# Bias and selection mask of a sparse attention added on TensorE by a product with the identity

## The chip, the cores and the metric

The kernel runs on one core of one Trainium2 chip. The metric is the device time of one execution in microseconds (us); the number given for a kernel is the median of several runs. The engines are called PE (TensorE, with PEld for its weight loads), DVE (VectorE), ACT (ScalarE), POOL (GpSimd) and SP (SyncE).

## The reference, cut to what matters

Two transformer blocks follow one another on 512 tokens of width 1024. The second has a sparse attention of 8 heads over a shared latent of 128 values. For each query the 128 keys with the best index score are selected, a bias by distance is added to the logits, and keys not selected or not causal are masked:

```python
logits = (einsum('bqhc,bqkc->bqhk', ql, c_sel) * ATT_SCALE + bias)
logits = where(valid[:, :, None, :], logits, -inf)
probs = softmax(logits, axis=-1)
return einsum('bqhk,bqkc->bqhc', probs, c_sel)
```

The kernel computes this densely: all causal keys of a block of 128 queries take part, and a mask of 0 (selected) or a huge negative number (not selected) is added.

## The kernel before, in words

All matrices are kept transposed, with features in the 128 partitions and the 512 tokens (T) along the free axis. The large projections are products in three parts: each weight chunk is split by ACT into a rounded half w_hi (line 1197) and by DVE or POOL into the rest w_lo (POOL: line 655), and PE runs w_hi·a_hi, w_hi·a_lo and w_lo·a_hi (lines 765 to 767 for chunks that fill gaps in other work, 743 to 745 elsewhere). The work of every engine is in program order, with semaphores between engines.

The change lies in the loop over the steps of the sparse attention, from 1187 to 1282 us of the span. There are 32 steps a = 0 to 31: 8 heads h = a // 4 times 4 query blocks i = a % 4. Block i has (i+1)·128 keys, so that the width of a step goes 128, 256, 384, 512. Each engine walks the same loop with a lag of its own:

- POOL (lines 696 to 714): one add per step makes bias_mask = t_bias + score for step a (line 708). There are two buffers, held in the tiles sum_sq and diagonal, so step a waits until step a-2 has been used. t_bias is loaded by a DMA that ACT issues, once per head (line 1455). Behind the add stands, in some steps, the split of a weight unit (w_lo, line 655).
- PE (lines 1052 to 1092): the logits of step a (line 1059, into one of three rotating "aux" banks), then the transposes of the probabilities of step a-2 (line 1066, i+1 blocks, which wait for DVE's attn2), then one or two chunks of a gate projection that fill the time (765 to 767; a third product closes a tile and releases one unit of weights), then the products with the values of step a-3 (line 1080), and in four steps (11, 19, 27, 35) the products of line 1090.
- DVE (lines 2278 to 2318): the add of step a, logit = bank + bias_mask (line 2286), which also sets the bank free; the reciprocal of the sum of step a-1 (2291); the maximum of logit of step a (2294) and its negation (2295), for which ACT waits; the scaling attn2 = prob · 1/sum of step a-1 (2303), for which PE's transposes of the next step wait.
- ACT (lines 1525 to 1560): the copy of the transposed probabilities of step a-2 (1530), the exponential of step a with its sum (1538, it is followed by a short row that reads the accumulator), then w_hi of a unit whose tile has closed, the copy of that tile (1470), and once per head the copy of the head's output (1552).

The aux banks are handed out in the order in which PE uses them: logit a, turn2 a-2 (the transposes), logit a+1, turn2 a-1, and so on, with an entry "ya" at the four steps of line 1090. An entry may be written when the entry three places before has been read. So turn2 a-1 takes the bank of logit a, and after a "ya" entry logit a+1 takes the bank of logit a.

Before the loop DVE selects the keys of block 1 (16 rounds of line 2205 and 2206, up to 1187 us), and POOL ends the splits of the units before (the last one runs from 1184.67 us). After the loop comes a recurrence in which DVE, ACT, POOL and PE take turns, filled with further chunks of the gate projection.

Of the kernel before, what the change touches and what calls it, by code (L numbers as in the profile page):

```python
# [34 lines left out]
ALU = mybir.AluOpType  # L35
# [3 lines left out]
P = 128  # L39
T = 512  # L40
# [277 lines left out]
def two_blocks(nc, ins, spill, bias_rows, out):  # L318

    with ExitStack() as ctx:  # L320
# [109 lines left out]
        qa = r2_under("qa", [P, 2, T])  # L430
        relu = r2_under("relu", [P, 2, T])
        i_t = r2_under("i_t", [P, 2, T])
        logit = r2("logit", [P, 2, T])
        prob2 = r2("prob2", [P, 2, T])
        attn2 = r2("attn2", [P, 2, T])
        after_steps = r2.at[0]
# [80 lines left out]
        def sem(name):  # L517
            return ctx.enter_context(nc.semaphore(name))
# [48 lines left out]
        spill_out = [sem(f"spill_out{i}") for i in range(2)]  # L567
        bias_in = [sem(f"bias_in{i}") for i in range(2)]
        logit_max = sem("logit_max")
        exp2_done = sem("exp2_done")  # L570
        attn2_ready = sem("attn2_ready")
        hq_loaded = [sem(f"hq_loaded{i}") for i in range(2)]
        hf_loaded = [sem(f"hf_loaded{i}") for i in range(2)]
# [74 lines left out]
        @block.gpsimd  # L648
        def _(pool):
            def split_unit(u, size, it=0, per_loop=0):  # L650
                slot, half = u % SLOTS, u % SLOTS
                hi, lo, src = w_hi[:, half, 0:size], w_lo[:, half, 0:size], raw[:, slot, 0:size]

                pool.wait_ge(unit_high, u + 1 + it * per_loop)
                pool.tensor_tensor(lo, src, hi.bitcast(F32), ALU.subtract).then_inc(unit_split, 1)  # L655

            def split_units(name, start, end):

                first, size = UNIT[name][0], UNIT[name][2] * P
                loops = max(0, end - start) // SLOTS  # L660
                if loops > 1:
                    with pool.Fori(0, loops) as it:
                        for j in range(SLOTS):
                            split_unit(first + start + j, size, it, SLOTS)
                    start += SLOTS * loops
                for i in range(start, end):
                    split_unit(first + i, size)

            def split_for(t):

                u = UNIT["proj2"][0] + t + 3
                split_unit(u, BLOCKS_OF[u] * P)

            def make_diff(e):

                h, l = e // len(LEVELS), e % len(LEVELS)
                b = LEVELS[l]
                if l == 0:
                    pool.wait_ge(sums_ready, h + 1)
                if e >= 2:  # L680
                    pool.wait_ge(decay_ready, decays((e - 2) // len(LEVELS), (e - 2) % len(LEVELS)))
                src = run[h % 2][:, max(0, l - 6), :].rearrange("p (n c) -> p n c", c=2 * b)
                to = diff[:, e % 2, :].rearrange("p (n c) -> p n c", c=2 * b)
                mid = src[:, :, b - 1:b].broadcast_to([P, T // (2 * b), b])
                ins_ = pool.tensor_tensor(to[:, :, 0:b], mid, src[:, :, 0:b], ALU.subtract)
                if b <= 32:
                    ins_ = pool.tensor_tensor(to[:, :, b:2 * b], src[:, :, b:2 * b], mid, ALU.subtract)
                ins_.then_inc(diff_ready, 1)

            split_units("proj1", 0, UNIT["proj1"][1])  # L690
            split_units("wo", 0, SLOTS)
            pool.wait_ge(unit_split, UNIT["proj2"][0] + SLOTS)
            split_units("proj2", SLOTS, LEAD2 + 3)

            pool.wait_ge(const2_loaded, 16 * 3)
            pool.wait_ge(rstd_ready, STAT["kidx"] + 1)
            for a in range(DSA_STEPS + 4):
                if a < DSA_STEPS:
                    h, i = a // QB, a % QB
                    end, first_col = (i + 1) * P, (QB - 1 - i) * P  # L700
                    if i == 0:
                        pool.wait_ge(bias_in[h % 2], 16 * (h // 2 + 1))
                    if a == 1:
                        pool.wait_ge(selected_ready, 3)
                    if a >= 2:
                        former = aux_read("logit", a - 2)
                        pool.wait_ge(former[0], former[1])
                    pool.tensor_tensor(bias_mask[a % 2][:, 0:end], t_bias[:, h % 2, first_col:first_col + end],
                                       score[i][:, :], ALU.add).then_inc(bias_mask_ready, 1)
                if a >= 3:  # L710
                    for t in closed(FILL2[a - 3]):
                        split_for(t)

            make_diff(0)
            for e in range(HGRN_STEPS):
                if e + 1 < HGRN_STEPS:
                    make_diff(e + 1)
# [3 lines left out]
        def _(pe):  # L721
# [331 lines left out]
            for a in range(DSA_STEPS + 4):  # L1053
                if a < DSA_STEPS:
                    h, i = a // QB, a % QB
                    end = (i + 1) * P
                    dst = aux_wait("logit", a)
                    wait(aux_read("qlat", h))
                    mm(dst[:, 0:end], qlat[:, h, i * P:end], ckv[:, 0:end], start=True,
                       stop=True).then_inc(aux_ready, 1)  # L1060
                if 2 <= a < DSA_STEPS + 2:
                    b = a - 2
                    dst = aux_wait("turn2", b)
                    pe.wait_ge(attn2_ready, b + 1)
                    for j in range(b % QB + 1):
                        step = pe.transpose(dst[:, j * P:(j + 1) * P], attn2[:, b % 2, j * P:(j + 1) * P],
                                            ident[:, :])
                    step.then_inc(aux_ready, 1)
                if a < DSA_STEPS + 3:
                    fill("proj2", FILL2[a])  # L1070
                if 3 <= a < DSA_STEPS + 3:
                    b = a - 3
                    h, i = b // QB, b % QB
                    if i == 0:
                        wait_bank("olat", h)
                        wait(aux_read("ckvtok", 0))
                    wait(aux_read("turn2", b))
                    dst = tile_bank("olat", h)
                    for j in range(i + 1):
                        step = mm(dst[:, i * P:(i + 1) * P], ckv_tok[:, j, :],  # L1080
                                  attn2_t[:, b % 2, j * P:(j + 1) * P], start=(j == 0), stop=(j == i))
                    if i == QB - 1:
                        step.then_inc(head_ready, 1)
                if a >= 11 and a % 8 == 3:
                    t = (a - 11) // 8
                    dst = aux_wait("ya", t)
                    wait(tile_read("olat", 2 * t))
                    wait(tile_read("olat", 2 * t + 1))
                    for n in range(2):
                        step = mm(dst[64 * n:64 * n + 64, :], wuv[:, 2 * t + n, :], olat[:, n, :], start=True,  # L1090
                                  stop=True)
                    step.then_inc(aux_ready, 1)
# [92 lines left out]
        def _(act):  # L1185
# [339 lines left out]
            for a in range(DSA_STEPS + 4):  # L1525
# [6 lines left out]
                if a < DSA_STEPS:  # L1532
# [2 lines left out]
                    act.wait_ge(logit_max, a + 1)  # L1535
                    if a >= 2:
                        act.wait_ge(attn2_ready, a - 1)
                    fn(prob2[:, a % 2, 0:end], logit[:, a % 2, 0:end], ACT.Exp,
                       bias=small[:, 24 + a % 2:25 + a % 2],
                       accum_out=small[:, 26 + a % 2:27 + a % 2]).then_inc(exp2_done, 1)  # L1540
                    if i == 1 and 1 <= h < DSA_HEADS - 1:
                        act.wait_ge(bias_mask_ready, QB * h)
                        load_bias(h + 1)
# [168 lines left out]
        def _(dve):  # L1712
# [565 lines left out]
            for a in range(DSA_STEPS + 4):  # L2278
                if a < DSA_STEPS:
                    h, i = a // QB, a % QB  # L2280
                    end, s = (i + 1) * P, a % 2
                    dve.wait_ge(bias_mask_ready, a + 1)
                    dve.wait_ge(aux_ready, AUX["logit", a] + 1)
                    if a >= 2:
                        dve.wait_ge(exp2_done, a - 1)
                    v.tensor_tensor(logit[:, s, 0:end], aux_bank("logit", a)[:, 0:end], bias_mask[s][:, 0:end],
                                    ALU.add).then_inc(aux_sem("logit", a), 1)
                if 1 <= a <= DSA_STEPS:
                    r = (a - 1) % 2
                    dve.wait_ge(exp2_done, a)  # L2290
                    step(v.reciprocal(small[:, 28 + r:29 + r], small[:, 26 + r:27 + r]))
                if a < DSA_STEPS:
                    wait(aux_read("logit", a))
                    step(v.tensor_reduce(small[:, 6:7], logit[:, s, 0:end], AX_X, ALU.max))
                    v.tensor_scalar(small[:, 24 + s:25 + s], small[:, 6:7], -1.0, None, ALU.mult).then_inc(
                        logit_max, 1)
                if 1 <= a <= DSA_STEPS:
                    b = a - 1
                    end, s = (b % QB + 1) * P, b % 2
# [250 lines left out]
```

## Time and profile before

| | before |
|---|---|
| median of 3 runs | 1962.74 us (1958.37 to 1964.58) |
| time of the profiled execution | 1960.72 us |
| its span | 1958.6 us |
| PE busy | 1836.3 us (94% of the span) |
| PEld busy | 1486.7 us (76%) |
| DVE busy | 1140.8 us (58%) |
| ACT busy | 657.1 us (34%) |
| POOL busy | 204.5 us (10%) |
| mean granted clock of TensorE | 0.972 |

A busy share is time in which at least one instruction of the engine is recorded as running. Matmuls are pipelined: a row of PE begins when the operands begin to stream in, and its recorded end overlaps with the next row, so the time that a matmul takes from the engine is read from the distance between two starts. The stage of the change takes 95 us of the 1958.6.

### The profile page before, as it was taken

The page shows a single profiled execution, that of the slowest core. Times are in us where ns is not written, and L with a number is a line of the kernel's source. Part 1 is how long each engine was busy: PE and PEld are TensorE (multiplying, and loading weights), DVE is VectorE, ACT ScalarE, POOL GpSimd, SP SyncE. Part 2 cuts the span into 40 slices and gives each one's busy share as a digit, 9 for nine tenths or more (in the row PEclk, how much of TensorE's full clock was granted, in tenths as well). Part 3 has the DMA queues.
Part 4 walks back from the last instruction along what each step waited for, and adds up shares of the span by engine and source line. Part 5 has one row for each costly group of instructions (what it writes and reads, how often), then busy time and mean ns, then how long its engine had stood idle before and what let it go on. Part 6 is the DMA issues. An engine that isn't in the chain of part 4 may idle for free.

```text
span 1958.6 us, 23662 instructions
## 1 busy us (share of the span) xinstructions
PE 1836.3 (94%) x8380; PEld 1486.7 (76%) x8380; DVE 1140.8 (58%) x1721; ACT 657.1 (34%) x978; POOL 204.5 (10%) x150
## 2 busy tenths in 40 slices
PE   6996999999999999999999998888898999999986
PEld 4675888888888888888776776667776888888864
DVE  6466668888334655532343777788666655552256
ACT  4333422333223222222333334444444322232242
POOL 3221000000000000000023334444000000000000
PEclk9997999999999999999899999999999999999998
DMA  4676222223322232333222333221241323332221
GB/s 141 71 75 49 86 97 96 96 96 104 102 91 79 97 96 96 100 103 104 80 76 76 105 123 118 69 88 43 93 153 56 108 96 96 96 119 101 90 67 54
DMA packets 55460, 180.62 MB, mean 92 GB/s; under 512 B 6336, under 2 KB 7104, under 8 KB 55392
## 3 DMA queue, kind: packets, MB, share of 16 engines
q1 hardware_dynamic: 43200, 157.07, 24.3%
q10 hardware_dynamic: 12192, 22.67, 7.2%
q8 instruction: 40, 0.66, 0.1%
q14 instruction: 28, 0.23, 0.0%
HBM read 167.65 MB, written 12.06 MB: 92 GB/s over the span
## 4 chain that ended last, share of the span: by engine, by line
PE 77%; DVE 14%; ACT 3%; issue 3%; DMA 2%; ACTq 0%; DVEq 0%; SPq 0%; POOL 0%
PE bank L743 20%; PE bank L744 20%; PE bank L745 20%; PE bank L765 2%; PE bank L767 2%; PE bank L766 2%; PE bank L839 2%; PE bank L840 1%; PE bank L841 1%; DVE score L2206 1%; DMA raw<-in_w_proj 1%; DVE best L2205 1%; PE bank L814 1%; PE bank L1132 1%; DVE chunk L1872 1%
## 5 line engine op out<-in xcount | busy, mean ns | idle before, releaser
L1197 ACT ACTIVATE w_hi<-raw 128x1024 fp32r<-128x1024 f32 (+2 forms) x281 | 304.6, 1087 | 743.7 <-PE bank L745 640.8
L743 PE MATMUL bank<-a_hi,w_hi 128*128 128x512 f32 x1272 | 500.6, 394 | 14.6 <-DVE w_lo L1775 4.9
L745 PE MATMUL bank<-a_hi,w_lo 128*128 128x512 f32 x1272 | 496.6, 390 | 0.0
L744 PE MATMUL bank<-a_lo,w_hi 128*128 128x512 f32 x1272 | 496.6, 390 | 0.0
L1775 DVE TENSOR_TENSOR w_lo<-raw,w_hi 128x1024 fp32r<-128x1024 f32 (+2 forms) x219 | 280.4, 1281 | 253.8 <-ACT w_hi L1197 241.2
L743 PEld LDWEIGHTS bank<-a_hi,w_hi 128*128 128x128 f32 x1272 | 239.7, 188 | 76.8 <-issue 18.9
L745 PEld LDWEIGHTS bank<-a_hi,w_lo 128*128 128x128 f32 x1272 | 239.6, 188 | 50.7
L744 PEld LDWEIGHTS bank<-a_lo,w_hi 128*128 128x128 f32 x1272 | 240.0, 189 | 48.8
L655 POOL TENSOR_TENSOR w_lo<-raw,w_hi 128x1024 fp32r<-128x1024 f32 x54 | 130.0, 2408 | 1071.3 <-ACT w_hi L1197 1071.3
L743 PE MATMUL bank<-h_hi,w_hi 128*128 128x512 f32 x568 | 221.0, 389 | 0.0
L744 PE MATMUL bank<-h_lo,w_hi 128*128 128x512 f32 x568 | 221.0, 389 | 0.0
L745 PE MATMUL bank<-h_hi,w_lo 128*128 128x512 f32 x568 | 220.9, 389 | 0.0
L745 PEld LDWEIGHTS bank<-h_hi,w_lo 128*128 128x128 f32 x568 | 106.6, 188 | 22.2
L743 PEld LDWEIGHTS bank<-h_hi,w_hi 128*128 128x128 f32 x568 | 106.6, 188 | 22.2
L744 PEld LDWEIGHTS bank<-h_lo,w_hi 128*128 128x128 f32 x568 | 106.6, 188 | 22.1
L765 PE MATMUL bank<-a_hi,w_hi 128*128 128x512 f32 x234 | 104.9, 448 | 3.4 <-ACT unrot L1311 3.4
L2123 DVE TENSOR_TENSOR val<-bank,rstd 128x512 f32<-128x512 f32 x44 | 30.4, 691 | 114.3 <-PE bank L745 114.3
L767 PE MATMUL bank<-a_hi,w_lo 128*128 128x512 f32 x234 | 95.1, 406 | 0.0
L766 PE MATMUL bank<-a_lo,w_hi 128*128 128x512 f32 x234 | 95.0, 406 | 0.0
L839 PE MATMUL bank<-a_hi,w_hi 128*128 128x512 f32 x150 | 64.9, 433 | 30.2 <-DVE a_lo L1781 28.6
L839 PEld LDWEIGHTS bank<-a_hi,w_hi 128*128 128x128 f32 x150 | 30.3, 202 | 43.6 <-DVE a_lo L1781 27.8
L840 PE MATMUL bank<-a_lo,w_hi 128*128 128x512 f32 x150 | 61.9, 413 | 0.0
(297 smaller groups left out, 2210.6 us busy)
## 6 DMA issues: line engine op xcount, KB each, us to landing
raw<-in_w_up SPq DMA_DIRECT2D x132, 512.0 KB, 3.4
raw<-in_w_down SPq DMA_DIRECT2D x48, 704.0 KB, 4.1
raw<-in_w_proj SPq DMA_DIRECT2D x59, 512.0 KB, 3.5
raw<-in_w_wo SPq DMA_DIRECT2D x8, 512.0 KB, 4.8
raw<-in_w_branch SPq DMA_DIRECT2D x16, 256.0 KB, 2.8
gates_in<-spill ACTq DMA_DIRECT2D x16, 256.0 KB, 3.2
raw<-in_w_out SPq DMA_DIRECT2D x8, 512.0 KB, 3.9
raw<-in_w_ple SPq DMA_DIRECT2D x8, 512.0 KB, 3.4
```

The lines of the kernel that those rows point to most:

```text
L655: pool.tensor_tensor(lo, src, hi.bitcast(F32), ALU.subtract).then_inc(unit_split, 1)
L743: mm(dst[:, :], wh, hi[:, k, :], start=(first and c == 0), stop=False)
L744: mm(dst[:, :], wh, lo[:, k, :], start=False, stop=False)
L745: step = mm(dst[:, :], wl, hi[:, k, :], start=False, stop=(last and c == n - 1))
L765: mm(dst[:, :], wh, a_hi[:, c, :], start=(c == 0), stop=False)
L766: mm(dst[:, :], wh, a_lo[:, c, :], start=False, stop=False)
L767: step = mm(dst[:, :], wl, a_hi[:, c, :], start=False, stop=(c == DC - 1))
L839: mm(dst[:, :], wh, hi[:, k, :], start=(k == 0), stop=False)
L840: mm(dst[:, :], wh, lo[:, k, :], start=False, stop=False)
L1197: fn(w_hi[:, slot, 0:size], raw[:, slot, 0:size], ACT.Copy).then_inc(unit_high, 1)
L1775: v.tensor_tensor(w_lo[:, slot, 0:size], raw[:, slot, 0:size], w_hi[:, slot, 0:size].bitcast(F32), ALU.subtract).then_inc(unit_split, 1)
L2123: v.tensor_tensor(val[:, :], bank[u][:, :], rstd[:, :], ALU.mult).then_inc(bank_free[u], 1)
```

## The change

POOL, PE, DVE and ACT are touched. On PE the logits of line 1059 are left open in the bank, and a second product, with the identity as the stationary and bias_mask as the moving operand, is added to the same bank. DVE has no add any more and takes the maximum straight from the bank; ACT's exponential reads the bank too and now sets it free. The tile logit is gone (its room stays reserved). POOL's wait for the buffer of step a-2 is now for PE's product instead of DVE's add. On DVE the maximum and its negation now stand ahead of the reciprocal.

```diff
@@ POOL
                     if a >= 2:
-                        former = aux_read("logit", a - 2)
-                        pool.wait_ge(former[0], former[1])
+                        pool.wait_ge(aux_ready, AUX["logit", a - 2] + 1)
@@ PE
                     wait(aux_read("qlat", h))
-                    mm(dst[:, 0:end], qlat[:, h, i * P:end], ckv[:, 0:end], start=True,
+                    mm(dst[:, 0:end], qlat[:, h, i * P:end], ckv[:, 0:end], start=True, stop=False)
+                    pe.wait_ge(bias_mask_ready, a + 1)
+                    mm(dst[:, 0:end], ident[:, :], bias_mask[a % 2][:, 0:end], start=False,
                        stop=True).then_inc(aux_ready, 1)
@@ ACT
-                    fn(prob2[:, a % 2, 0:end], logit[:, a % 2, 0:end], ACT.Exp,
+                    fn(prob2[:, a % 2, 0:end], aux_bank("logit", a)[:, 0:end], ACT.Exp,
                        bias=small[:, 24 + a % 2:25 + a % 2],
-                       accum_out=small[:, 26 + a % 2:27 + a % 2]).then_inc(exp2_done, 1)
+                       accum_out=small[:, 26 + a % 2:27 + a % 2]).then_inc(aux_sem("logit", a), 1)
@@ DVE
-                    dve.wait_ge(bias_mask_ready, a + 1)
                     dve.wait_ge(aux_ready, AUX["logit", a] + 1)
+                    step(v.tensor_reduce(small[:, 6:7], aux_bank("logit", a)[:, 0:end], AX_X, ALU.max))
                     if a >= 2:
-                        dve.wait_ge(exp2_done, a - 1)
-                    v.tensor_tensor(logit[:, s, 0:end], aux_bank("logit", a)[:, 0:end], bias_mask[s][:, 0:end],
-                                    ALU.add).then_inc(aux_sem("logit", a), 1)
+                        wait(aux_read("logit", a - 2))
+                    v.tensor_scalar(small[:, 24 + s:25 + s], small[:, 6:7], -1.0, None, ALU.mult).then_inc(
+                        logit_max, 1)
                 if 1 <= a <= DSA_STEPS:
                     r = (a - 1) % 2
-                    dve.wait_ge(exp2_done, a)
+                    wait(aux_read("logit", a - 1))
                     step(v.reciprocal(small[:, 28 + r:29 + r], small[:, 26 + r:27 + r]))
-                if a < DSA_STEPS:
-                    wait(aux_read("logit", a))
-                    step(v.tensor_reduce(small[:, 6:7], logit[:, s, 0:end], AX_X, ALU.max))
-                    v.tensor_scalar(small[:, 24 + s:25 + s], small[:, 6:7], -1.0, None, ALU.mult).then_inc(
-                        logit_max, 1)
```

## Rows read from the trace of the kernel before

**Rows 1.** Windows: us, busy (rows) of each engine, granted clock, DMA share, GB/s

```profile
1187.00:1282.00 95.00, 79.88 (x430) 61.06 (x430) 66.89 (x171) 46.52 (x116) 37.61 (x37) 0.95 0.24 82
...
1187.00:1196.40 9.40, 5.39 (x15) 3.59 (x16) 6.68 (x21) 2.93 (x9) 4.54 (x7) 0.64 0.04 14
...
1230.47:1240.66 10.19, 10.19 (x57) 7.55 (x58) 7.42 (x21) 4.72 (x13) 3.90 (x5) 1.00 0.12 34
...
1261.90:1275.87 13.97, 10.67 (x54) 8.39 (x52) 9.26 (x21) 6.00 (x16) 4.74 (x3) 0.88 0.05 20
```

**Rows 2.** Waits, 1187 to 1282 us: us in total, times, longest us

```profile
PE bank L1066 <- DVE attn L2303: 15.6, 11, 4.4
```

**Rows 3.** Timeline of PE, steps 7 and 8: start us, us, line, operation, [idle before]

```profile
1203.17 1.02 PE L1059 MATMUL bank<-ckv,qlat 128*128 128x512 f32 x2
1204.03 0.38 PE L1066 MATMUL bank<-ident,attn 128*128 128x128 f32 x2
1204.17 0.48 PE L765 MATMUL bank<-a_hi,w_hi 128*128 128x512 f32 x1
...
1204.95 0.38 PE L1080 MATMUL bank<-attn_t,ckv_tok 128*128 128x128 f32 x2
1205.17 0.39 PE L1059 MATMUL bank<-ckv,qlat 128*128 128x128 f32 x2
1206.57 0.52 PE L1066 MATMUL bank<-ident,attn 128*128 128x128 f32 x3 [1.01 <-DVE attn L2303]
```

**Rows 4.** Timeline of DVE, ACT and POOL in the same steps

```profile
1204.40 0.69 DVE L2286 TENSOR_TENSOR logit<-bank,diagonal 128x512 f32<-128x512 f32 x1 [0.87 <-PE bank L1059]
...
1205.19 0.69 DVE L2294 TENSOR_REDUCE small<-logit 128x1 f32<-128x512 f32 x1
...
1206.00 0.42 DVE L2303 TENSOR_SCALAR attn<-prob,small 128x384 f32<-128x384 f32 x1
...
1207.91 2.67 DVE L2303 TENSOR_SCALAR attn<-prob,small 128x512 f32<-128x512 f32 x1
...
1206.10 0.73 ACT L1538 ACTIVATE prob<-logit,small 128x512 f32<-128x512 f32 x1 [1.27 <-DVE small L2295]
...
1206.83 1.04 ACT L1197 ACTIVATE w_hi<-raw 128x1024 fp32r<-128x1024 f32 x1
...
1206.56 0.46 POOL L708 TENSOR_TENSOR sum_sq<-t_bias,tri 128x128 f32<-128x128 f32 x1 [5.39 <-DMA t_bias<-bias_rows]
...
1207.95 2.34 POOL L655 TENSOR_TENSOR w_lo<-raw,w_hi 128x1024 fp32r<-128x1024 f32 x1 [0.22 <-ACT w_hi L1197]
```

**Rows 5.** Groups by shape: busy us, mean ns

```profile
L2286 DVE TENSOR_TENSOR logit<-bank,diagonal 128x512 f32<-128x512 f32 x8 | 5.5, 692 | 9.3 <-PE bank L1059 9.3
L2294 DVE TENSOR_REDUCE small<-logit 128x1 f32<-128x512 f32 x8 | 5.5, 686 | 0.3
...
L1538 ACT ACTIVATE prob<-logit,small 128x512 f32<-128x512 f32 x8 | 5.8, 724 | 8.7 <-DVE small L2295 8.7
```

**Rows 6.** The same, in the first attention, which reads its banks directly

```profile
L1988 DVE TENSOR_REDUCE small<-bank 128x1 f32<-128x512 f32 x8 | 5.5, 692 | 1.9 <-PE bank L956 1.7
...
L1334 ACT ACTIVATE prob<-bank,small 128x512 f32<-128x512 f32 x8 | 5.5, 688 | 14.6 <-DVE small L1989 14.3
```

**Rows 7.** Timeline at the start of the loop: PE, then POOL

```profile
1185.38 0.81 PE L1059 MATMUL bank<-ckv,qlat 128*128 128x384 f32 x2
1190.59 0.45 PE L1066 MATMUL bank<-ident,attn 128*128 128x128 f32 x1 [4.41 <-DVE attn L2303]
...
1195.60 0.39 PE L1059 MATMUL bank<-ckv,qlat 128*128 128x128 f32 x2
...
1186.99 0.51 POOL L708 TENSOR_TENSOR sum_sq<-t_bias,tri 128x128 f32<-128x128 f32 x1
```

**Rows 8.** Timeline of steps 28 and 29: PE's wait, DVE's scaling before it

```profile
1266.03 0.63 PE L1066 MATMUL bank<-ident,attn 128*128 128x128 f32 x4 [2.06 <-DVE attn L2303]
...
1263.60 2.28 DVE L2303 TENSOR_SCALAR attn<-prob,small 128x512 f32<-128x512 f32 x1
```

More of the change, by code:

```diff
@@ L432, in two_blocks @@
         i_t = r2_under("i_t", [P, 2, T])
-        logit = r2("logit", [P, 2, T])
+        r2.at[0] += 2 * T * 4
         prob2 = r2("prob2", [P, 2, T])
@@ L569, in two_blocks @@
         logit_max = sem("logit_max")
-        exp2_done = sem("exp2_done")
         attn2_ready = sem("attn2_ready")
```

## The prediction

> **What bounds the kernel now.** I read the page first (PE is busy in all but 6% of the span), then the windows of the stage that is changed, its waits, and the timeline of each engine in it. The windows show two things [rows 1]. Over the stage's 95 us the recorded PE time is 79.9 us, more than DVE's 66.9, ACT's 46.5 or POOL's 37.6. And there is a head, 1230.47 to 1240.66 us, in which PE's rows touch one another for all 10.19 us. The waits name one thing that PE waits for: DVE's attn2 ahead of the transposes, 15.6 us in 11 waits, the longest (4.4 us) at the start of the loop [rows 2]. So the stage is PE's own work, with ten waits of 11.2 us together behind a chain on DVE and one longer wait at the start. PE's clock fell in two places: 0.64 granted in the first 9.4 us, and 0.88 in the last 13.97 us [rows 1], which is 13.97 · 0.12 = 1.7 us lost.
>
> The chain behind a wait, in steps 7 and 8 [rows 4]: logits of step 7 end, add 0.69, reciprocal, maximum 0.69, negation, attn2 of step 6 0.42, and only then PE's transposes at 1206.57 [rows 3]. The gap shown is 1.01, but by starts it is 1206.57 - 1205.17 less the 0.22 that a product of 128 columns takes, so 1.2. Corrected so (some 0.17 for each of ten), the ten waits are worth 12.9 us.
>
> **The change, part by part.**
>
> *The product with the identity (PE, on the path).* It has the shape of the product of line 1059. That one takes 1204.03 - 1203.17 = 0.86 us for 512 columns, two rows [rows 3], so 0.215 for each 128. A head adds 1 + 2 + 3 + 4 = 10 such pieces, 2.15 us; steps 4 to 31 add 7 · 2.15 = **+15.05 us**. A head without waits goes from 10.19 to 12.3. Bounds: if it ran in one row for each block, as the transposes with the identity do (1204.17 - 1204.03 = 0.14 for two blocks [rows 3], or 0.07; other transposes of the trace take up to 0.11), it would be half, +7.5; above, half clock as in the first stretch would double what falls into it. I take 0.215, since the moving operand is not transposed and the instruction is that of line 1059 but for its operands.
>
> *The add that goes (DVE).* 0.69 us at 512 columns [rows 5], less at fewer (0.29 at 128). It is off the path where PE doesn't wait; where it does, the chain is shorter by the add of the step before. *Maximum and exponential from the bank:* the first attention does just that. The maximum takes 692 ns there against 686, the exponential 688 against 724 [rows 5, 6]. Both count as nothing (between -0.04 and +0.01 each).
>
> *Which of the waits are left.* PE comes later to its transposes by the new products, DVE is ready earlier. From the end of the products of a step with 512 columns, attn2 of the step before was ready after 1206.57 - 1204.03 = 2.5 us [rows 3]. Without the add it would be 1.8. But the transposes also need the bank of that step's logits, and it now comes free after the exponential: latency 0.35, maximum 0.7, negation and hand-over 0.3, exponential with its accumulator 0.85, so 2.2 to 2.3 us. PE meanwhile has two transposes, a chunk, and values, logits and mask of a 128 step: 1205.17 - 1204.03 = 1.14, and 2 · 0.22, so 1.57. A wait of **0.7** stays, in steps 4, 8, 16, 24 and 32, 3.5 us. In steps 12, 20 and 28 the products of line 1090 stand before it and cover it. The waits in steps 9, 21, 13 and 22 go: PE arrives later by 0.66 to 1.1 us and DVE is ready 0.3 to 0.7 sooner.
>
> *POOL's splits.* attn2 of step 7 took 2.67 us for 512 columns beside a POOL split of 2.34 [rows 4], and in step 28 2.28 [rows 8]; it seems to wait the split out. The split follows ACT's exponential and w_hi (exponential at 1206.10, w_hi 1206.83, split 1207.95 [rows 4]). With the change exponential and split are both 0.7 earlier against the logits. For step 7 I get attn2 from 2.6 to 3.1 us behind the products and the split from 3.35, so no collision (by 0.25 us); for step 28, where DVE copies ya first, attn2 still falls into the split, and a wait of about **1.2** is left of 2.06 [rows 8]. Left in all: 3.5 + 1.2 = 4.7 of 12.9, so **-8.2 us**.
>
> *Clock.* With the wait of step 29 down to 1.2, what PE did before the fall in the last stretch is gone; I count the **-1.7**, and 0 as the other end.
>
> *The start.* This is the new wait. Before, PE ran logits 0 to 2 with their chunks up to 1186 us, while DVE was still selecting, and then stood until 1190.59. Now it stands in front of the first mask product until POOL's first add at 1186.99 + 0.51 = 1187.5 [rows 7]; behind it in PE's queue stand all chunks, logits 1 and 2 and the first transposes. They were done for nothing before. PE has stood 4 us, so I take it to run at half clock for some 4.5 us behind it again: the 0.64 over the first 9.4 us [rows 1] is 6.8 us at half clock, part of it standing. Then: mask 0 0.44, chunk 1.28, logits and mask 1 1.76, chunk 1.28, logits and mask 2 1.3 at full clock, transposes of step 0 at 1193.6, chunk, logits and mask 3 to 1196.1, transposes, chunk, values, logits and mask 4 to 1197.65. Logits 4 ended at 1195.8 before [rows 7]. Less the 0.22 of mask 4, already counted, that is **+1.6 us** (bounds: 0 if the clock stays up, +3).
>
> *POOL's new wait.* It starts its add 0.3 us sooner behind the logits than behind DVE's add, and PE needs the result two steps later, 5 us. Hidden. The one tight place is mask 8: its bias arrived after 5.39 us of waiting, at 1206.56 [rows 4], after PE's logits 8 but before its next transposes. The loads stand behind four others that ACT issues in step 4, which comes 1.5 us later now, and PE reaches mask 8 at some 1209.0, POOL has it at 1208.5. Hidden by half a microsecond; if not, PE stands here with everything behind it.
>
> *Sum:* 15.05 - 8.2 - 1.7 + 1.6 = +6.75, about **+7 us**. On the profiled execution's 1960.72 us that is 1967.7. It lies 2 us below the median of 1962.74, so that the forecast for a median is **1969.7 us**.
>
> **Rivals.**
>
> *PE has room (not slower).* All ten waits vanish and the start costs nothing: the new products fall into time in which PE stood. Then 15.05 - 12.9 - 1.7 = +0.5, 1963 us. It decides where the bank comes free before PE arrives, that is if the exponential of a 512 step ends within 1.6 us of its products instead of 2.3. For it speaks that weight loads fill only 61.06 of 95 us [rows 1]. The Trainium skill (Perfetto Trace Analysis, Identifying the Most-Contended Engine) would have PE's headroom judged by the share of weight loads and by arithmetic, not by matmul busy time; by that PE would have a third to spare and the change would fit in. Against it speaks the head of 10.19 us: weight loads are 7.55 us of it, 74%, and yet no row of PE starts late [rows 1]. Chance 0.27.
>
> *Half-price product (not slower).* One row instead of two, -7.5 from the sum: 1962. Chance 0.05.
>
> *PE stands for POOL or ACT (much slower).* The mask comes late in PE's queue: mask 8 behind its DMA, or a mask behind a split of 2.3 us; or ACT, with w_hi, the tile copy and the head's copy in one step (1.0 + 0.6 + 0.6), starts the next exponential late and holds the bank. Each such place costs 1 to 2 us where it hits, and four or five steps have a split: +6 more, and the fallen clock is not won back (+1.7). 1975 to 1978 us. For it: the long wait of POOL for its DMA [rows 4]; against it: two steps of lead. Chance 0.14.
>
> *DVE's chain rules the stage (faster).* Only if waits were due in most steps; then the 15.6 us of adds would come off and the products would be in the shade: -7 us. The gap-free head speaks against it. Chance 0.04.
>
> **How the numbers follow.** The forecast, +4 to +10 us, has 0.5 of the chance. 0.3% of this kernel, 5.9 us, is about what its runs can tell from no change, and lies just below the sum. Of the forecast some two thirds lie above it; the first two rivals lie within it, the third above. That gives slower 0.56, same 0.39, faster 0.05. The range goes from 1963 (PE has room) to 1976 (forecast plus a few places where PE stands); the forecast's own range is 1966.5 to 1973.
>
> **What the profile would show.** The product of the new line as two rows of 0.43 each for 512 columns, some 17 us of starts in all. PE's stretch from the first transposes of head 1 to those of head 7 longer by about its share. The wait of line 1066 down from 15.6 us in 11 to some 5 in 6, in steps with i = 0, and put down to ACT's exponential as much as to attn2. A new wait of PE of about 4 us for POOL at 1183.6. The last logits products of the loop ending near 1281 instead of 1273. I would be wrong if DVE's waits on the path outlast the removed add (collisions with POOL at new places), if the clock falls anew, or if the mask product shows waits for POOL after step 3.

## The result, and the profile after

The changed kernel takes 1965.74 us as the median of 16 runs (1962.59 to 1968.82), the kernel before 1962.44 us in 16 runs beside it (1956.13 to 1964.58). The ratio is 1.0025, with a 95% interval of 1.0014 to 1.0036: slower by 5 us, 3 to 7 (the two medians alone are 3.3 us apart). The prediction was +7, a median of 1969.7 and a range of 1963 to 1976.

The windows of the changed kernel, for the 95 us of the stage and for the 103 that it takes now (columns as in rows 1):

```profile
1187.00:1282.00 95.00, 90.49 (x463) 67.19 (x464) 44.10 (x134) 41.47 (x108) 39.28 (x37) 0.98 0.24 83
1187.00:1290.00 103.00, 97.14 (x504) 72.83 (x504) 50.07 (x145) 47.53 (x118) 39.28 (x37) 0.98 0.24 82
```

Against [rows 1], over the whole stage (95 us before, 103 now), DVE fell from 66.9 to 50.1 us and PE rose from 79.9 to 97.1. The engine with room lost work and the one without got it. The granted clock of the stage rose from 0.95 to 0.98: the fall in the last stretch is gone, the one at the start has stayed (below).

The waits of the changed kernel from 1175 to 1290 us, those that bear on PE and on the new hand-overs:

```profile
POOL sum_sq L706 <- DMA t_bias<-bias_rows: 11.4, 5, 4.9
...
PE bank L1059 <- POOL sum_sq L706: 3.8, 1, 3.8
...
PE bank L1066 <- DVE attn L2298: 1.2, 2, 0.7
PE bank L1066 <- ACT prob L1538: 1.1, 4, 0.3
```

PE's waits at the transposes, 15.6 us in 11 before [rows 2], are 2.3 in 6 (1.2 and 1.1 in the last two lines). In their place stands one wait of 3.8 us for POOL. Here it is in PE's timeline, with the first transposes and what runs at half clock between them:

```profile
1185.31 0.38 PE L1057 MATMUL bank<-ckv,qlat 128*128 128x128 f32 x2
1189.50 0.49 PE L1059 MATMUL bank<-sum_sq,ident 128*128 128x128 f32 x2 [3.81 <-POOL sum_sq L706]
...
1190.96 1.05 PE L1057 MATMUL bank<-ckv,qlat 128*128 128x256 f32 x2
1191.81 1.06 PE L1059 MATMUL bank<-diagonal,ident 128*128 128x256 f32 x2
...
1195.00 0.27 PE L1066 MATMUL bank<-ident,attn 128*128 128x128 f32 x1
...
1198.66 0.39 PE L1057 MATMUL bank<-ckv,qlat 128*128 128x128 f32 x2
```

A product of 256 columns takes 1191.81 - 1190.96 = 0.85 us here, 0.43 later. The windows say why (columns as in rows 1, first a stretch of the changed kernel, then its loop behind the start, then the last stretch of the kernel before):

```profile
1190.00:1193.00 3.00, 3.00 (x8) 2.36 (x8) 0.47 (x3) 0.46 (x2) 1.16 (x3) 0.50 0.00 0
1198.90:1291.00 92.10, 87.74 (x473) 66.11 (x471) 44.88 (x125) 44.19 (x109) 32.69 (x30) 1.00 0.25 84
...
1266.03:1270.00 3.97, 3.97 (x16) 3.44 (x17) 1.98 (x5) 1.09 (x3) 1.96 (x2) 0.60 0.02 4
```

The granted clock is 0.50 there, the lower level of 1.2 GHz, shortly after PE stood for 3.8 us. Behind the start it is 1.00 up to 1291 us. Before, it was 0.60 once more in the 4 us behind the wait of step 29 [rows 8]. Steps 7 and 8 in the changed kernel, PE:

```profile
1207.39 1.02 PE L1057 MATMUL bank<-ckv,qlat 128*128 128x512 f32 x2
1208.26 1.02 PE L1059 MATMUL bank<-diagonal,ident 128*128 128x512 f32 x2
1209.11 0.38 PE L1066 MATMUL bank<-ident,attn 128*128 128x128 f32 x2
...
1210.25 0.39 PE L1057 MATMUL bank<-ckv,qlat 128*128 128x128 f32 x2
1210.47 0.39 PE L1059 MATMUL bank<-sum_sq,ident 128*128 128x128 f32 x2
1211.13 0.55 PE L1066 MATMUL bank<-ident,attn 128*128 128x128 f32 x3 [0.27 <-ACT prob L1538]
```

And DVE, ACT and POOL beside them:

```profile
1209.38 0.69 DVE L2283 TENSOR_REDUCE small<-bank 128x1 f32<-128x512 f32 x1 [2.21 <-PE bank L1059]
...
1211.55 0.49 DVE L2298 TENSOR_SCALAR attn<-prob,small 128x512 f32<-128x512 f32 x1
...
1210.30 0.69 ACT L1538 ACTIVATE prob<-bank,small 128x512 f32<-128x512 f32 x1 [0.38 <-DVE small L2286]
1210.88 0.19 ACT L1538 ACTIVATION_READ_ACCUMULATOR prob<-bank,small 128x1 f32 x1
...
1209.09 0.46 POOL L706 TENSOR_TENSOR sum_sq<-t_bias,tri 128x128 f32<-128x128 f32 x1 [4.95 <-DMA t_bias<-bias_rows]
...
1212.10 2.36 POOL L654 TENSOR_TENSOR w_lo<-raw,w_hi 128x1024 fp32r<-128x1024 f32 x1 [1.86 <-ACT w_hi L1197]
```

The new product takes 1209.11 - 1208.26 = 0.85 us for 512 columns, and 0.22 for 128 (from 1223.63 to the next start at 1223.85). The transposes after it wait 0.27 by the row (0.44 by starts), and what they wait for is ACT's exponential, which sets the bank free at 1211.07. attn2 of step 7 runs at 1211.55 in 0.49 us, against 2.67 before [rows 4]; it is done before POOL's split starts at 1212.10.

To leave out what happens ahead of the stage I take times from the first logits (1183.33 us before, 1185.31 after) to the last products of line 1090 (1283.70 and 1291.25): 100.4 us before, 105.9 after, **+5.6 us**. The 2 us between the two starting points are no part of the change. Over the twelve profiles of the versions below, whose code up to there is the same on PE, the first logits start anywhere from 1181.4 to 1186.8. The time from those last products to the end of the span scatters too, from 673 to 678 us.

### The profile page after: what moved, and what is told of

Its sections match the earlier page's. It is cut to its first block, busy times and chain, and to the rows that moved or that the text cites. A ratio compares the mean times of both kernels' runs of the same rounds, so it can differ in the third digit from the quotient of the medians.

```text
span 1965.1 us, 23727 instructions
## 1 busy us (share of the span) xinstructions
PE 1852.9 (94%) x8444; PEld 1498.4 (76%) x8444; DVE 1121.5 (57%) x1689; ACT 656.4 (33%) x978; POOL 204.1 (10%) x150
## 4 chain that ended last, share of the span: by engine, by line
PE 79%; DVE 12%; ACT 3%; issue 3%; DMA 2%; POOL 0%; ACTq 0%; DVEq 0%; SPq 0%; POOLq 0%
PE bank L741 20%; PE bank L742 20%; PE bank L743 20%; PE bank L763 2%; PE bank L764 2%; PE bank L765 2%; PE bank L837 2%; PE bank L838 1%; PE bank L839 1%; DMA raw<-in_w_proj 1%; PE bank L812 1%; PE bank L779 1%; DVE chunk L1872 1%; DVE x L1874 1%; PE bank L1132 1%
```

## The experiments

All stand on one of the two kernels. "Stretch" is the time just defined, from the run's own profile. Each ratio is to runs of the kernel before on the same chip. The runs were made on several chips (the kernel before had medians from 1960.8 to 1963.1 on them), so medians of different rows are compared more safely by their ratios.

| run | median us | ratio to before, 95% interval | stretch us |
|---|---|---|---|
| before | 1962.44 | | 100.4 |
| changed | 1965.74 | 1.0025 (1.0014 to 1.0036) | 105.9 |
| e1 changed, no product | 1951.35 | 0.9942 (0.9925 to 0.9960) | 91.8 |
| e2 changed, logits twice | 1980.26 | 1.0092 (1.0061 to 1.0123) | 121.1 |
| e3 before, logits twice | 1969.34 | 1.0040 (1.0021 to 1.0059) | 108.6 |
| e4 changed, mask 0 early | 1963.85 | 1.0008 (0.9990 to 1.0027) | 106.1 |
| e5 before, scaling first | 1955.36 | 0.9965 (0.9951 to 0.9979) | 95.6 |
| e5b the same again | 1955.70 | 0.9968 (0.9953 to 0.9983) | 96.3 |
| e6 changed, scaling first | 1965.03 | 1.0020 (1.0005 to 1.0035) | 105.8 |
| e7 changed, mask in fp32r | 1956.95 | 0.9975 (0.9963 to 0.9986) | 96.4 |
| e8 e7, mask 0 early | 1956.78 | 0.9970 (0.9954 to 0.9986) | 97.8 |
| e9 e7, scaling first | 1957.24 | 0.9970 (0.9959 to 0.9982) | 96.6 |
| e10 e8, loads later | 1956.84 | 0.9980 (0.9967 to 0.9993) | 98.0 |
| e11 e4, loads later | 1965.85 | 1.0022 (1.0009 to 1.0035) | 106.0 |

Ratio and stretch do not always give the same difference to the kernel before. For e3 they agree (+7.8 us and +8.2). For e1 they are -11.4 and -8.6, for e8 -5.9 and -2.6, for e4 +1.6 and +5.7. The stretch is one profile of each version, and e5 and e5b, the same code, differ by 0.7 us in it. So what is said below of single microseconds rests on single waits in single profiles.

### e1: the product taken out

The logits get neither bias nor mask here, so the kernel leaves out a part of the work; PE's wait for the mask goes with the product.

```diff
-                    mm(dst[:, 0:end], qlat[:, h, i * P:end], ckv[:, 0:end], start=True, stop=False)
-                    pe.wait_ge(bias_mask_ready, a + 1)
-                    mm(dst[:, 0:end], ident[:, :], bias_mask[a % 2][:, 0:end], start=False,
-                       stop=True).then_inc(aux_ready, 1)
+                    mm(dst[:, 0:end], qlat[:, h, i * P:end], ckv[:, 0:end], start=True,
+                       stop=True).then_inc(aux_ready, 1)
```

> The changed kernel without the product with the identity and without its wait for the mask; the logits get neither bias nor mask, POOL's adds still run. Theory A (PE's own time rules the stage, the product costs 0.215 us for each 128 columns): some 12 us under the changed kernel, and 8 us under the kernel before, since the add's share of the waits is gained and nothing is paid: PE's waits in the loop fall from 12.9 us to 6 or 7, the fallen clock of the last stretch is not there, so about 1954 us. Rival B (PE has room, the product falls into its waits): within 2 us of the changed kernel, 1963 to 1966. Rival D (DVE's chain rules): also about the changed kernel.

Measured: 1951.35 us, 14.4 under the changed kernel and 11 under the one before by the medians. PE's waits in it, 1175 to 1300 us:

```profile
PE bank L1065 <- DVE attn L2297: 6.5, 5, 3.2
...
PE bank L1065 <- ACT prob L1537: 1.5, 3, 0.6
```

The product and its wait for the mask cost 105.9 - 91.8 = 14.1 us of the stretch, where the product takes 17.2 from PE; so it is not hidden. The other half of the change, the add off DVE and both reads from the bank, is worth 8.6 us by itself (100.4 to 91.8). About 1.6 of them are the clock, which is 1.00 in the last 28 us of e1's stretch and was 0.60 for 4 us before. I had expected 12 and 8.

### e2 and e3: PE's share doubled on both kernels

```diff
+                    mm(dst[:, 0:end], qlat[:, h, i * P:end], ckv[:, 0:end], start=True, stop=True)
...
```

> The changed kernel with the product of the logits issued twice (the second overwrites the first): PE gets 8 times 2.15 = 17.2 us more, nothing else changes. Theory A: hardly a wait is left to take it up (some 3 us), so +13 to +16 us on the changed kernel, 1979 to 1982. Rival B: under +5.

> The kernel before with the product of the logits issued twice: the change's price on PE without what it takes from DVE, from POOL's order and from the start. Theory A: 17.2 us more, of which 2 fall into the standing time at the start, about 5 into the ten waits, and 1.7 come back from the clock: +8 to +10, 1971 us, so 4 to 5 us above the changed kernel, which is what the add on DVE is worth less the new wait at the start. Rival B: the waits of 12.9 us take it all up, +2. Rival D: +2 as well, since the chain on DVE is as long as before.

e2 took 14.5 us more than the changed kernel. From the first logits to the last transposes its profile has 114.8 us against 99.6, so 15.2 of the 17.2 us are paid. e3 took 6.2 us more than the kernel before by the medians, 7.8 by the ratio and 8.2 by the stretch. The waits there take up the other half: the same work added on PE costs 8 us where PE has 11 us of waits in the loop, and 15 where it has 2. e3 has PE's part of the change without DVE's, and lies 2.6 us of stretch above the changed kernel: that is what the add on DVE is worth once PE is full, net of the new wait at the start. I had expected 4 to 5.

### e4: the mask of step 0 ahead of POOL's last split

```diff
-            split_units("proj2", SLOTS, LEAD2 + 3)
+            split_units("proj2", SLOTS, LEAD2 + 2)
...
+            pool.wait_ge(bias_in[0], 16)
+            pool.tensor_tensor(bias_mask[0][:, 0:P], t_bias[:, 0, (QB - 1) * P:QB * P], score[0][:, :],
+                               ALU.add).then_inc(bias_mask_ready, 1)
+            split_units("proj2", LEAD2 + 2, LEAD2 + 3)
             for a in range(DSA_STEPS + 4):
-                if a < DSA_STEPS:
+                if 0 < a < DSA_STEPS:
```

> The changed kernel with POOL's add of step 0 ahead of its last split before the loop, so that PE's first mask product finds its mask. Theory A: PE's wait of 3.8 us shrinks, it goes on to logits 1 and then waits for mask 1, which can only follow the selection that DVE ends at about 1187: 1 to 2 us less than the changed kernel, 1964 to 1965. If the start cost nothing (rival B): no difference.

The median is 1963.85, but the stretch is no shorter. PE's waits in it, 1175 to 1300 us:

```profile
PE bank L1063 <- POOL diagonal L710: 2.9, 1, 2.9
...
PE bank L1070 <- DVE attn L2302: 2.1, 3, 0.8
PE bank L1070 <- ACT prob L1542: 0.9, 3, 0.3
PE bank L1063 <- POOL sum_sq L710: 0.6, 1, 0.6
```

The first transposes come 8.7 us after the first logits instead of 9.7. The gain of 1 us is given back in step 8, where PE now stands 0.6 us for mask 8 (the last row), whose bias comes by DMA, and another 0.8 for attn2 in the step after. So the early mask shortens the wait at the start by 0.9 us, from 3.8 to 2.9, and later steps lose that again. A start without any wait was not tried. The interval of e4's ratio overlaps that of the changed kernel: within the measurement the two are the same.

### e5 and e6: DVE's scaling ahead of its add or maximum

```diff
+                if 1 <= a <= DSA_STEPS:
+                    r = (a - 1) % 2
...
+                    step(v.reciprocal(small[:, 28 + r:29 + r], small[:, 26 + r:27 + r]))
...
+                    v.tensor_scalar(attn2[:, s, 0:end], prob2[:, s, 0:end], small[:, 28 + s:29 + s], None,
+                                    ALU.mult).then_inc(attn2_ready, 1)
                 if a < DSA_STEPS:
                     h, i = a // QB, a % QB
...
-                    step(v.reciprocal(small[:, 28 + r:29 + r], small[:, 26 + r:27 + r]))
...
-                    v.tensor_scalar(attn2[:, s, 0:end], prob2[:, s, 0:end], small[:, 28 + s:29 + s], None,
-                                    ALU.mult).then_inc(attn2_ready, 1)
```

> The kernel before with DVE's reciprocal and scaling of step a-1 ahead of its add of step a, so that the transposes never wait for the add and the maximum. If the add and the maximum ahead of attn2 are the whole of the ten waits, they go: -10 us, 1952. But the loop then has DVE and ACT in one ring (exponential, reciprocal, scaling, add, maximum, negation, exponential): by the rows some 3.0 + 0.8 + 3.0 + 1.95 + 1.95 + 0.6 us for a head and 1.2 of hand-overs, 12.5 us, against 10.2 of PE's own work and 11.3 measured. By that it is slower, up to +9, 1971. I hold the second for likelier.

> The changed kernel with the same order on DVE. The ring without the add is 10.5 us for a head, under PE's 12.3, so it doesn't rule. Theory A says that the waits that are left in steps 4, 8, 16, 24 are for the bank, which ACT's exponential frees, not for attn2: then nothing changes, within 1.5 us of the changed kernel. If they were for attn2 they would go: -2 us.

e5 is 6.5 us faster than the kernel before, and I had held it for slower. The groups of the scaling by shape in e5, 1183 to 1280 us:

```profile
L2289 DVE TENSOR_SCALAR attn<-prob,small 128x512 f32<-128x512 f32 x8 | 4.6, 571 | 0.6 <-PE bank L1059 0.3
...
L2289 DVE TENSOR_SCALAR attn<-prob,small 128x128 f32<-128x128 f32 x8 | 3.0, 374 | 0.3
```

and in the kernel before, 1183 to 1282 us:

```profile
L2303 DVE TENSOR_SCALAR attn<-prob,small 128x512 f32<-128x512 f32 x8 | 9.3, 1160 | 0.0
L2303 DVE TENSOR_SCALAR attn<-prob,small 128x128 f32<-128x128 f32 x8 | 8.5, 1067 | 0.0
```

Wherever in the fourteen profiles no row of POOL is beside it, a scaling takes 0.29, 0.35, 0.42 or 0.49 us, by its width. Longer rows stand only where a row of POOL overlaps. Before, 19 of the 32 scalings overlap one, all eight of 128 columns among them; in e5 it is 8 of 32, and all scalings together fall from 24.7 to 14.0 us.

My sum for the ring of DVE and ACT, 12.5 us for a head, was too long. The scalings of 512 and 128 columns take (1160 - 571) + (1067 - 374) ns = 1.3 us of it away, which leaves 11.2, but two heads, from 1236.05 to 1256.36, take 10.2 us each, PE's own time [rows 1]. Summing recorded lengths counted too much: the scaling at 1238.37 is recorded with 0.49 us, and the next row of DVE starts 0.40 after it.

Not all of the gain comes from POOL. Of the ten waits of the loop before, six (7.5 us) stand behind a scaling that overlaps POOL, and four (3.7 us) behind one of 0.42 us that overlaps nothing; there the add and the maximum stand ahead of the scaling, as in steps 7 and 8 [rows 4]. The clock is 1.00 in e5's last 27 us, which is worth another 1.6. How the gain divides among the three was not measured. By the stretch it is 4.8 us, and 4.1 in e5b, not 6.5; where the rest lies is open. e5b, with the kernel before run beside it again, confirms the time:

> The kernel before with the scaling ahead of the add once more, on the same chip as the run beside it, to tell which of the two is faster. From its first run 1955.4; the same within 2 us as the run beside it.

In e6 the same order brings nothing (105.8 against 105.9 us of stretch), as expected. Of PE's waits that are left in the changed kernel those of 0.3 us in steps 4, 8, 16 and 24 are for the bank. In e6 they are 0.2, and in step 8 it is the mask that comes last. The two for attn2, 1.2 us in steps 29 and 32, do go, but PE then stands 1.2 us for the bank in step 29.

### e7 to e9: a cheaper product

The mask buffers and a copy of the identity are typed fp32r (the mask and the bias are rounded so), and the product has one row instead of two:

```diff
-                    mm(dst[:, 0:end], ident[:, :], bias_mask[a % 2][:, 0:end], start=False,
+                    mm(dst[:, 0:end], ident_r[:, :], bias_mask[a % 2][:, 0:end], start=False,
```

> The changed kernel with mask and identity held as fp32r, so that the product takes one pass of 0.23 us for 512 columns as those of lines 763 to 765 do, and not 0.86 (the mask and the bias are rounded so far). Theory A: PE gets 8 times 0.57 us and some 0.1 us for each change of kind, 7.8 us in place of 17.2; some waits come back. 1956 to 1959 us, 7 to 9 under the changed kernel and under the one before too. Rival C (PE stands for POOL or ACT in these steps): no gain, since the waits would stay.

> The same, and POOL's add of step 0 ahead of its last split as well. Theory A: 1 to 2 us under the run before it, 1955 to 1957.

> The changed kernel with the mask product in fp32r and with DVE's reciprocal and scaling ahead of the maximum. In the fp32r kernel PE still waits for attn2 3.3 us in 4 waits and for the bank 1.3 us in 3 inside the loop. Theory A: the scaling, moved ahead, no longer falls into POOL's splits, the waits for attn2 go and those for the bank stay or grow a little: 1 to 3 us under it, 1954 to 1956. If the waits for attn2 turn into waits for the bank: no difference.

PE's timeline of steps 7 and 8 in e7:

```profile
1201.38 1.02 PE L1062 MATMUL bank<-ckv,qlat 128*128 128x512 f32 x2
1201.84 0.80 PE L1066 MATMUL bank<-bias_mask,ident_r 128*128 128x512 f32 x1
1202.47 0.38 PE L1073 MATMUL bank<-ident,attn 128*128 128x128 f32 x2
```

Logits and mask take 1.09 us together where they took 1.72: the mask's part is 1.09 - 0.86 = 0.23. The kernel is 8.8 us faster than the changed one and 5 faster than the one before. That is the prediction's sum with one term exchanged, and the best evidence that this term was the price. By starts the mask's part is 0.23, 0.17, 0.12 and 0.06 us for the four widths, so 4.6 us in eight heads in place of 17.2. PE's waits by the rows grow from 6.1 to 9.0, and 12.6 - 2.9 = 9.7 is what the stretch shows: 105.9 - 96.4 = 9.5. e8 and e9 bring nothing more in the median, and e8's stretch is 1.5 us longer: in e8 the microsecond won at the start is lost to a wait of 1.8 us for mask 8, in e9 the waits for attn2 (3.3 us in 4) become waits for the bank (3.5 us in 6).

### e10 and e11: the loads out of the way of mask 8

```diff
-                if a == 4:
+                if a == 6:
```

> The fp32r kernel with mask 0 early, and ACT's six loads of step 4 (resets, masks, two forget and two query tiles) issued in step 6, behind the load of the bias of head 2 instead of ahead of it. Theory A: in the run without this PE stood 1.8 us for mask 8, whose bias comes behind these loads; that wait goes, 1 to 2 us less, about 1955. Rival: the 1.1 us won at the start are lost to the waits for the bank and for attn2, whatever mask 8 does: then no difference and no wait for POOL in step 8.

> The changed kernel (product in full precision) with mask 0 early and the same loads in step 6. PE's waits of 0.62 for mask 8 and of 0.82 for attn2 in step 9 (0.28 of bank time in the changed kernel) go back: PE's stretch from the first logits to the last products of line 1090 is 105.0 us instead of 106.1, about 1964 us.

Both missed. The wait for mask 8 went, and PE's waits in e11, 1175 to 1300 us, have it in another place:

```profile
PE bank L1063 <- POOL diagonal L710: 3.0, 1, 3.0
...
PE bank L1070 <- ACT prob L1542: 2.0, 4, 1.1
PE bank L1070 <- DVE attn L2302: 1.2, 2, 0.7
```

What holds the bank is ACT. Here are its rows in e10 (ACTq is its queue as it issues a DMA) and PE's wait:

```profile
1205.80 0.34 ACTq L1565 DMA_DIRECT2D resets<-in_c_resets  x1
...
1209.22 0.63 ACTq L1525 DMA_DIRECT2D hq<-spill  x1
1209.90 0.38 ACT L1541 ACTIVATE attn_t<-bank 128x256 f32<-128x256 f32 x1 [3.52 <-issue]
1210.18 0.68 ACT L1549 ACTIVATE prob<-bank,small 128x512 f32<-128x512 f32 x1
...
1211.01 0.55 PE L1077 MATMUL bank<-ident,attn 128*128 128x128 f32 x3 [2.75 <-ACT prob L1549]
```

The six loads are issued from 1205.80 to 1209.85. DVE's negation for step 7 had run at 1207.68, but the exponential starts only at 1210.18. So now the exponential of step 7 comes late and holds the bank: 1.1 us in e11, 2.75 in e10. The issues take ACT's queue 4.0 us in e10, 3.2 in e11 and 3.1 in the kernel before (1197.50 to 1200.57). The cost of the bundle is ACT's time in this loop. A place for it outside the loop was not tried.

## Why the prediction was right

The direction, the cause and most terms held. The total of +7 was 1 to 2 us too high, by the stretch (+5.6) and by the ratio (+5). The median of 1965.74 lies 4 us under the 1969.7 forecast and just under the forecast's own range, 1966.5 to 1973; it is inside the wide range that the rivals had made.

- *The product on PE.* 0.215 us for each 128 columns, forecast from line 1059, measured 0.85 for 512. Right, and e1, e2 and e7 show that it is the price: 14.1 to 15.2 us of the 17.2 are paid. The half-price rival is out: the product is two rows.
- *The waits that are left.* Forecast 0.7 in each of steps 4, 8, 16 and 24, covered in 12, 20 and 28, by the bank and not by attn2. Measured 0.44 by starts in exactly those four, put down to ACT's exponential. I had put the bank's release at 2.2 to 2.3 us behind the products; it is 1211.07 - 1209.11 = 1.96. The last one (step 32) is 0.7 as forecast, that of step 29 0.9 instead of 1.2, and 0.3 came up in step 9. In all 3.6 instead of 4.7 of 12.9. This was the mis-sized term.
- *The collisions with POOL's split.* attn2 of step 7 was to be done at 3.1 us behind the products and the split to start at 3.35; it is 2.93 and 2.99. Right in sign by 0.06 us, which is luck: it could have gone the other way. In step 28 attn2 fell into the split as forecast (2.06 us from 1272.18, beside the split at 1271.58).
- *The clock.* The fall in the last stretch is gone: the granted clock is 1.00 from 1198.90 to 1291.00. Whether the shorter wait in step 29 alone did it is not shown.
- *The start.* Forecast a wait of 4 us and a loss of 1.6; measured 3.8 and, at the end of mask 4 against logits 4, 13.8 - 12.5 us from the first logits less the 0.22 of mask 4, so 1.1. The clock was back after 3.6 us, not 4.5.
- *Sum by measured terms.* 15.05 - 9.3 - 1.7 + 1.1 = 5.2, against 5.6 in the stretch.
- *The chances.* They do not follow from their parts. Two thirds of 0.5 and the third rival's 0.14 make 0.47 for slower, not 0.56, and what is left for the same is 0.49, not 0.39.
- *PE has room.* Out, by e1 and e2. With it goes the reading by weight loads: they are 72.83 of 103 us in the changed kernel, 71%, where PE's waits are 3.8 + 2.3 us. The Trainium skill (Perfetto Trace Analysis, Identifying the Most-Contended Engine) takes this share, beside the arithmetic done, as the measure of PE's headroom. This case's traces do not agree: a product of 512 columns in two rows of 0.43 us needs a weight load of 0.19 for each, and the share stays low with PE full.
- *PE stands for POOL or ACT.* Beyond the start and the short waits for the bank it did not come in the changed kernel: mask 8 was ready at 1209.55, the product ran at 1210.47. The loads issued in step 4 are six, not the four of the prediction. But e4, e8, e10 and e11 show it behind the next door.
- *DVE's chain rules the stage.* Out in this form: with the adds gone the kernel is slower. What I did not see is how much of the ten waits came from the order of DVE's work, behind the add and the maximum and into POOL's rows. e5 changes that order and takes 4 to 5 us off the stretch without any work for PE.

## What to carry to other kernels

Work that moves from an engine with gaps to the engine without them has to be paid there, here 14 to 15 us of 17, and is repaid only by the waits that it removes; count both from the starts of rows, head by head, and look for a stretch without any gap to know what full is. Before moving an operation, try its order: the add could stay on DVE, and the scaling moved ahead of it gave 6.5 us by the medians, 4 to 5 in the stretch. If a mask is to be added by a product, use the cheapest form that its precision allows, one row instead of the two of full fp32.

## What the runs showed of the hardware that I had not expected

- DVE's scaling from SBUF to SBUF took 1160 ns on average for 512 columns and 1067 for 128 in the kernel before, and 571 and 374 in the order of e5; with no row of POOL beside it it takes 490 and 290. A row of 2.67 us began at 1207.91, before the POOL row at 1207.95 beside which it stood [rows 4]: the recorded start does not tell which of the two has to wait.
- Six DMA issues in a row took ACT's queue for 3.1 us in the kernel before, 3.2 in e11 and 4.0 in e10, longer than the exponentials of a whole head with their sums (some 3.0 us).
- The same code ahead of the loop brought the first logits anywhere from 1181.4 to 1186.8 us, so that a change of 5 us is better read from a stretch of its own than from spans.
